# Second feed-forward: two of three chunks of the first projection as seven half-size products

## The reference, cut to what matters

```python
def swiglu(h, w_in, w_out):
    gate, up = jnp.split(h @ w_in, 2, axis=-1)
    return ((jax.nn.silu(gate) * up) @ w_out).astype(h.dtype)
...
    h = h + swiglu(rms_norm(h, ffn_norm[i]), ffn_w_in[i], ffn_w_out[i])
    h = rms_norm(h, final_norm)
```

## Time and profile before

| | |
|---|---|
| three executions | 1677.31, 1680.96, 1684.79 us |
| the profiled execution: span | 1680.7 us (its own time is not given apart from the span; 0.3 below the median) |
| TensorE busy | 1640.0 us, 98% |
| VectorE busy | 919.1 us, 55% |
| ScalarE busy | 632.4 us, 38% |
| POOL busy | 92.6 us, 6% |
| HBM traffic | 101 GB/s over the span |
| first projection of the second feed-forward | 1304.15 to 1545.40 us of the span |

### The profile page before, as it was taken

How to read it: one execution, slowest core, us unless ns; L and a number is a source line. 1 busy time by engine, 2 the same in 40 slices (tenths; PEclk the granted TensorE clock), 3 DMA queues, 4 the chain that set the end, 5 groups by cost and what they waited for, 6 DMA issues and landing times.

```text
span 1680.7 us, 20208 instructions
## 1 busy us (share of the span) xinstructions
PE 1640.0 (98%) x7941; PEld 1333.0 (79%) x7941; DVE 919.1 (55%) x1262; ACT 632.4 (38%) x816; POOL 92.6 (6%) x130
## 2 busy tenths in 40 slices
...
GB/s 320 129 119 80 44 26 51 226 164 179 160 150 151 64 102 85 101 101 77 86 103 131 86 76 52 76 65 96 97 127 75 101 100 101 100 90 66 92 104 51
DMA packets 227365, 176.71 MB, mean 105 GB/s; under 512 B 15812, under 2 KB 213316, under 8 KB 227270
## 3 DMA queue, kind: packets, MB, share of 16 engines
...
HBM read 166.84 MB, written 2.13 MB: 101 GB/s over the span
## 4 chain that ended last, share of the span: by engine, by line
PE 83%; DVE 9%; ACT 4%; issue 1%; SPq 1%; DMA 1%; DVEq 0%; POOLq 0%; POOL 0%; ACTq 0%
PE PS L477 23%; PE PS L479 23%; PE PS L478 23%; PE PS L2393 2%; PE PS L486 1%; DVE WL L92 1%; DVE T L92 1%; DMA MODW<-in_w_mod 1%; PE PS L498 1%; PE PS L500 1%; PE PS L499 1%; SPq L2682 1%; PE PS L649 1%; ACT WH L88 1%; DVE SUMS L111 1%
## 5 line engine op out<-in xcount | busy, mean ns | idle before, releaser
L477 PE MATMUL PS<-XH,WH 128*128 128x512 f32 (+2 forms) x1264 | 481.1, 381 | 3.2 <-DVE WL L92 1.1
L478 PE MATMUL PS<-XL,WH 128*128 128x512 f32 (+2 forms) x1264 | 476.8, 377 | 0.0
L479 PE MATMUL PS<-XH,WL 128*128 128x512 f32 (+2 forms) x1264 | 476.8, 377 | 0.0
L92 DVE TENSOR_TENSOR WL<-WS,WH 128x2048 fp32r<-128x2048 f32 (+3 forms) x131 | 272.8, 2083 | 209.4 <-ACT WH L88 206.6
L477 PEld LDWEIGHTS PS<-XH,WH 128*128 128x128 f32 (+1 forms) x1264 | 236.0, 187 | 48.9 <-DVE WL L92 2.0
L479 PEld LDWEIGHTS PS<-XH,WL 128*128 128x128 f32 (+1 forms) x1264 | 235.9, 187 | 44.8
L478 PEld LDWEIGHTS PS<-XL,WH 128*128 128x128 f32 (+1 forms) x1264 | 236.0, 187 | 43.2 <-issue 0.7
L88 ACT ACTIVATE WH<-WS 128x2048 fp32r<-128x2048 f32 (+3 forms) x131 | 229.1, 1749 | 76.2 <-PE PS L479 46.7
L477 PE MATMUL PS<-HH,WH 128*128 128x512 f32 x352 | 137.2, 390 | 0.2 <-DVE WL L92 0.2
L478 PE MATMUL PS<-HL,WH 128*128 128x512 f32 x352 | 136.9, 389 | 0.0
L479 PE MATMUL PS<-HH,WL 128*128 128x512 f32 x352 | 136.9, 389 | 0.0
...
## 6 DMA issues: line engine op xcount, KB each, us to landing
WS<-in_w_in SPq DMA_DIRECT2D x24, 1024.0 KB, 5.4
...
WS<-in_fox_w_in SPq DMA_DIRECT2D x16, 1024.0 KB, 5.6
...
MODW<-in_w_mod SPq DMA_DIRECT2D x8, 1024.0 KB, 11.7
```

The source lines that it names most:

```text
L92: self.e.tensor_tensor(o, a, b, op).then_inc(*self.done.to(*key))
L477: e.matmul(o, lh, rh, start=first and i == 0, stop=False)
L478: e.matmul(o, lh, rl, start=False, stop=False)
L479: ins = e.matmul(o, ll, rh, start=False, stop=last and i == n - 1)
```

## The change

Of the 22 chunks the 14 whose number is no multiple of three (`SEVEN`) are computed as a 2 x 2 block product in Strassen's way: seven products of half the terms (4) and half the tokens (256) in place of eight. A chunk is four blocks in `WS` (`blocks`): two halves of the inner dimension by gate and up. POOL makes four sums of blocks (`sums_pool`), in two buffers of rows; ScalarE and VectorE make high and low parts by units (unit 0: one block; 1 and 2: two sums each; 3: two blocks), each unit in its own place of `WH` and `WL`, taken again as soon as its last product is done (`unit_free`). Four sums of the activations (`TS`, with parts `TSH`, `TSL`) are made by VectorE and ScalarE during the output projection. The seven results lie in halves of four PSUM banks; ScalarE copies the first, and VectorE forms the sums from PSUM (`PC`, `UG`). Only the gate half is multiplied by `RST`; the up half is left unscaled, and the second projection's results are multiplied by `RST` instead, by one more VectorE instruction per tile. The other eight chunks stay whole, in two units.

The new tiles lie where x and part of the hidden rows were: x is stored in DRAM when the output projection is done and read back for the second projection (`XPARK`), and the hidden rows 5 to 12 are stored (`HPARK`), their place is taken by rows 14 to 21, and they are read back to where the activations' sums were, in time for the sixth term of the second projection. SyncE's queue issues these transfers between the weight loads (`park_load`).

The diff, cut (left out are functions that only name a cell or pass a call on, and the second projection's TensorE and ScalarE programs, which differ from the ones before by the order of the first chunk's terms and the wait for the rows read back):

```diff
@@ -297,6 +297,21 @@
     QO = zone("QO", [128, 8, L], F32R, 0)
     KO = zone("KO", [128, 8, L], F32R, 16)
+    TSH, TSL = (zone(n, [128, 4, 4, 256], F32R, k) for n, k in (("TSH", 28), ("TSL", 72)))
+    TS = zone("TS", [128, 4, 4, 256], F32, 60)
+    SA = zone("SA", [128, 4, 512], F32, 52)
+    SB = zone("SB", [128, 4, 512], F32, 88)
+    UG = zone("UG", [128, 2, 512], F32, 96)
+    PC = zone("PC", [128, 3, 256], F32, 100)
+    XPARK = nc.dram_tensor("xpark", (128, 8 * L), F32, kind="Internal").ap()
+    HPARK = [nc.dram_tensor(f"hpark{i}", (128, 8 * L), F32, kind="Internal").ap() for i in range(2)]
+    def home(f):
+        return f if f < 14 else f - 9
+    def kept(f):
+        return f + 9 if 5 <= f < 13 else home(f)
     A1, AC, A2, QG, FINV, G12, RV = 0, 8, 16, 32, 40, 48, 56
     EPSC = 143
     ST = SM[:, 128:140]
...
@@ -368,7 +386,7 @@
         arrived.append(filled[slot(j)])
     def place(j):
-        return (j - RAW + (j > GATE) + (j > GATE + 1)) % 2
+        return (j - RAW + (j > GATE) + (j > GATE + 1) + (j >= DN2)) % 2
     def stage(j):
         nk, n = chunks[j][1:3]
@@ -385,6 +403,7 @@
     freed[GATE + 1] = ("w", GATE)
     freed[GATE + 2] = ("w", GATE + 1)
     freed[GATE + 3] = ("na_values", 7)
+    freed[DN2] = ("up2", 21, 1)
     def load_chunk(e, j):
@@ -401,6 +420,11 @@
             e.wait_ge(*pe.at("w", j - 4))
         else:
             e.wait_ge(*dve.at("wl", j - 3))
+        if UP2 <= j < DN2:
+            view = stage(j).rearrange("p (x k n) -> p x k n", x=2, k=nk)
+            for x, src in parts:
+                e.dma_start(view[:, x, :, :], src).then_inc(ws_in[slot(j)], 16)
+            return
         view = stage(j).rearrange("p (k n) -> p k n", k=nk)
         for c, src in parts:
...
+    UNIT_OF = {1: (0, 0), 6: (1, 0), 5: (1, 1), 7: (2, 0), 3: (2, 1), 4: (3, 1), 2: (3, 0)}
+    PLACE_OF = {1: (0, 0), 6: (0, 256), 5: (1, 0), 7: (1, 256), 3: (2, 0), 4: (2, 256), 2: (3, 0)}
+    SEVEN = [f for f in range(22) if f % 3]
+    def seven(f):
+        return f in SEVEN
+    def unit(w, f, b):
+        p1 = place(UP2 + 1)
+        if b == 0:
+            return w[:, p1, 1536:2048] if SEVEN.index(f) % 2 else w[:, p1, 0:512]
+        return (w[:, p1, 512:1536], w[:, 1 - p1, 0:1024], w[:, 1 - p1, 1024:2048])[b - 1]
...
+    def unit_free(f, b):
+        if f == 1:
+            return "w", (UP2 - 1 if b < 2 else UP2)
+        if b == 0:
+            s = SEVEN.index(f)
+            return ("up2", SEVEN[s - 2], 1) if s > 1 else ("w", UP2 - 1)
+        if b == 3:
+            return "up2", SEVEN[SEVEN.index(f) - 1], 2
+        return "up2", f - 1, (5, 3)[b - 1] if seven(f - 1) else b
+    def hi_unit(a, f, b):
+        if not seven(f) or b in (0, 3):
+            a.e.wait_ge(ws_in[slot(UP2 + f)], arrived[UP2 + f])
+        else:
+            a.e.wait_ge(*pool.at("up2_s", f, b))
+        a.e.wait_ge(*pe.at(*unit_free(f, b)))
+        a.act(unit_cells(WH, f, b), unit_source(f, b), ACT.Copy, key=("up2_wh", f, b))
+    def lo_unit(v, f, b):
+        v.e.wait_ge(*acts.at("up2_wh", f, b))
+        v.tt(unit_cells(WL, f, b), unit_source(f, b), unit_cells(WH, f, b).bitcast(F32), ALU.subtract,
+             key=("up2_wl", f, b))
+        if b == (3 if seven(f) else 2):
+            dve.name("wl", UP2 + f)
+    def sums_pool(g, f, b):
+        st = stage(UP2 + f).rearrange("p (a n) -> p a n", a=4)
+        S = sums_of(f)
+        if b == 1:
+            g.e.wait_ge(ws_in[slot(UP2 + f)], arrived[UP2 + f])
+        if f == 2 and b == 1:
+            g.e.wait_ge(*landed("x_out"))
+        if f > 1:
+            g.e.wait_ge(*dve.at("up2_wl", SEVEN[SEVEN.index(f) - 1], b))
+        if b == 1:
+            g.tt(S[:, 1, :], st[:, 2, :], st[:, 3, :], ALU.add)
+            g.tt(S[:, 0, :], S[:, 1, :], st[:, 0, :], ALU.subtract, key=("up2_s", f, 1))
+        else:
+            g.tt(S[:, 2, :], st[:, 2, :], st[:, 0, :], ALU.subtract)
+            g.tt(S[:, 3, :], st[:, 1, :], S[:, 0, :], ALU.subtract, key=("up2_s", f, 2))
...
+    def part_pe(e, f, p):
+        b, x = UNIT_OF[p]
+        wh, wl = (unit(w, f, b)[:, 512 * x:512 * x + 512] for w in (WH, WL))
+        rh, rl = rows_of(p)
+        tm = [(wh[:, 128 * k:128 * k + 128], wl[:, 128 * k:128 * k + 128], rh[:, k, :], rl[:, k, :]) for k in range(4)]
+        prod(e, part_bank(f, p), tm, ("up2", f, p))
...
+    def up2_pe(e):
+        w, wl = (t[:, place(UP2), :].rearrange("p (x k n) -> p x k n", x=2, k=8) for t in (WH, WL))
+        e.wait_ge(*dve.at("wl", UP2))
+        tm = [terms(w[:, m], wl[:, m], 0) for m in range(2)]
+        prod_by_rows(e, [whole_bank(0, 0), whole_bank(0, 1)], tm, lambda k: dve.at("norm4", "lo", k), ("up2", 0, 2))
+        e.wait_ge(*dve.at("norm4", "sum", 7))
+        pe.name("w", UP2)
+        sums_pe(e, "norm4", T[2], L, True, True, ("norm4", "sums"), step=1)
+        for f in range(1, 22):
+            if not seven(f):
+                for m in range(2):
+                    e.wait_ge(*dve.at("up2_wl", f, m + 1))
+                    if m == 0:
+                        e.wait_ge(*dve.at("up2_done", f - 2))
+                    whole_pe(e, f, m)
+                pe.name("w", UP2 + f)
+                continue
+            e.wait_ge(*dve.at("up2_wl", f, 0))
+            if f > 2:
+                e.wait_ge(*dve.at("up2_done", f - 2))
+            part_pe(e, f, 1)
+            e.wait_ge(*dve.at("up2_wl", f, 1))
+            if f == 1:
+                e.wait_ge(*dve.at("t_lo", 3))
+            part_pe(e, f, 6)
+            if f == 2:
+                e.wait_ge(*dve.at("up2_done", 0))
+            part_pe(e, f, 5)
+            e.wait_ge(*dve.at("up2_wl", f, 2))
+            part_pe(e, f, 7)
+            if f == 1:
+                spread_pe(e, "norm4", L)
+            part_pe(e, f, 3)
+            e.wait_ge(*dve.at("up2_wl", f, 3))
+            if f == 1:
+                e.wait_ge(*dve.at("t_fourth"))
+            part_pe(e, f, 4)
+            part_pe(e, f, 2)
+            pe.name("w", UP2 + f)
...
+    def up2_act(a):
+        hi_unit(a, 1, 0)
+        hi_unit(a, 1, 1)
+        root_act(a, "norm4", L, step=1)
+        hi_unit(a, 1, 2)
+        a.e.wait_ge(*dve.at("t_fourth_full"))
+        a.act(TSH[:, 0, :, :], TS[:, 3, :, :], ACT.Copy, key=("t_fourth_hi",))
+        for f in range(1, 22):
+            if seven(f):
+                if f > 1 and not seven(f - 1):
+                    hi_unit(a, f, 2)
+                hi_unit(a, f, 3)
+                if f > 1:
+                    up2_silu_act(a, f - 1)
+                if seven(f + 1):
+                    hi_unit(a, f + 1, 0)
+                up2_copy_act(a, f)
+                hi_unit(a, f + 1, 1)
+                if f == 1:
+                    a.e.wait_ge(*pe.at("norm4", "spread"))
+                    a.act(RST[:, 0:L], bank(3), ACT.Copy, key=("norm4", "inverse"))
+                    up2_silu_act(a, 0)
+                up2_hi_act(a, f - 1)
+                hi_unit(a, f + 1, 2)
+            else:
+                up2_silu_act(a, f - 1)
+                if f < 21:
+                    hi_unit(a, f + 1, 0)
+                up2_hi_act(a, f - 1)
+                if f < 21:
+                    hi_unit(a, f + 1, 1)
+                else:
+                    hi_chunk(a, DN2)
+        up2_silu_act(a, 21)
+        up2_hi_act(a, 21)
...
+    def up2_second_dve(v, f):
+        v.e.wait_ge(*acts.at("up2_copy", f))
+        if f == 1:
+            v.e.wait_ge(*landed("x_out"))
+        v.tt(PC[:, 0, :], part_bank(f, 6), first_copy(f), ALU.add)
+    def up2_third_dve(v, f):
+        v.e.wait_ge(*pe.at("up2", f, 7))
+        v.tt(PC[:, 1:3, :], part_bank(f, 5, 512).rearrange("p (x n) -> p x n", x=2),
+             PC[:, 0, :].unsqueeze(1).broadcast_to([128, 2, 256]), ALU.add)
+        v.tt(UG[:, 1, 256:512], part_bank(f, 5), PC[:, 2, :], ALU.add)
+    def up2_first_dve(v, f):
+        e = v.e
+        if not seven(f):
+            e.wait_ge(*pe.at("up2", f, 2))
+            if f == 0:
+                e.wait_ge(*acts.at("norm4", "inverse"))
+            v.tt(up2_tile(f), whole_bank(f, 1), RST[:, 0:L], ALU.mult, key=("up2_first", f))
+            return
+        e.wait_ge(*pe.at("up2", f, 4))
+        v.tt(UG[:, :, :].rearrange("p x n -> p (x n)")[:, 256:768], part_bank(f, 3, 512),
+             PC[:, 1:3, :].rearrange("p x n -> p (x n)"), ALU.add)
+        v.tt(up2_tile(f), UG[:, 1, :], RST[:, 0:L], ALU.mult, key=("up2_first", f))
+        e.wait_ge(*pe.at("up2", f, 2))
+        v.tt(UG[:, 0, 0:256], part_bank(f, 2), first_copy(f), ALU.add, key=("up2_done", f))
+    def up2_times_dve(v, f):
+        v.e.wait_ge(*acts.at("up2_silu", f))
+        v.tt(up2_tile(f), up2_tile(f), UG[:, 0, :] if seven(f) else whole_bank(f, 0), ALU.mult, key=("up2_times", f))
+        if not seven(f):
+            dve.name("up2_done", f)
...
+    def up2_dve(v):
+        e = v.e
+        lo_unit(v, 1, 0)
+        lo_unit(v, 1, 1)
+        diagonal_dve(v, "norm4", L)
+        lo_unit(v, 1, 2)
```

(143 more changed lines are left out.)

79 lines of the change are left out of this document (54 added, 25 removed).

## The result

The changed kernel takes 1690.39 us in the median of 13 executions (1680.04 to 1693.34), the kernel before 1678.52 in 13 on the same chip (1674.45 to 1685.15): ratio 1.0054, 95% interval 1.0034 to 1.0075. The ratios in this text are estimated from all executions of both kernels; the quotient of the two medians is 1.0071 here. So the change is slower, and whether by less or by more than the bound of 0.5% stays open, as the interval reaches to both sides of it. The profiled execution took 1692.03 us, its span is 1690.2.

The account below looks back on a forecast made before the run. The prediction took TensorE to bound the kernel (busy 98% of the span): 1680.7 - 13.5 saved + 12 at the start + 6.5 steady + 0.5 read-back + 0.7 end = 1687 us; own range 1680 to 1694, 8 in 10 1671 to 1702.

Parts of the forecast that it names:

- What TensorE saves: First projection: narrow matmuls spaced 0.118 us save 0.97 us in each of 14 chunks, 13.5 us (11.2 at 0.1200).
- Exclusion of POOL and VectorE: First projection: a POOL sum and a VectorE instruction with two SBUF operands exclude each other, both sides losing in turn.
- Ahead of chunk 0: Start of first projection: tiles 4 and 5 delay chunk 0's WL, so TensorE waits 1.6 us.
- Chunk 1: Start: POOL's sums alternate with VectorE's last low parts; first product waits 4.3 us, the next 1.0 more.
- Chunk 2: Start: third product waits 1.5 us for chunk 0's bank, fourth and sixth 1.6 and 1.9 for low parts.
- Steady part: Later chunks: low part for the second chunk's sixth product late; about 1.3 us per three chunks, five groups, 6.5 us.
- Read-back: Second projection: reading parked hidden rows back takes 14.5 us, 14.3 covered; cost put at 0.5 us, ends 0 and 3.
- End: Second projection: the norm's last multiplication stands between the final matmul and the last addition, 0.7 us.
- sums slip by: Rival, faster: POOL's sums mostly meet VectorE idle or on PSUM operands; 1674 us, at best 1671; chance 0.27.
- VectorE sets the pace: Rival, slower: each POOL sum stops VectorE for 1.28 us; 22 us in place of 6.5, 1702 us; chance 0.17.
- Narrow products save nothing: Rival: narrow matmul spacing rises to 0.1295 us, kernel 1700 us; its chance is inside the slower ones.
- parked rows or gaps dear: Rival, slower: read-back costs 3 to 6 us, or waits let the granted clock fall; 1692 us; chance 0.08.

Follow-up runs that it names:

- e1: Against the changed kernel, POOL's sums replaced by constant writes, four for two sums; first-projection stage 233.85 us against 249.27, one execution 1671.07 us.
- e7: Against the changed kernel, POOL's sums replaced by six constant writes per pair, as long as the sums; first-projection stage 235.04 us against 249.27.

## Why the prediction was right, and where its steps were not

The forecast was 1687 us with its own range of 1680 to 1694, and the median is 1690.4: the mechanism as laid, a saving on TensorE eaten by late low parts. Faster, same and slower stood at 0.17, 0.45 and 0.38, with "same" the likeliest, and the interval of the result lies across the bound between "same" and slower. In these two profiles the forecast's terms came to +6.2 us, the measured ones to +11.1, and the stage took 249.3 us for some 246. That the sum came this near is in part luck: single terms were off by 2.4, 3.8 and 0.8 us one way and by 1.6 and 0.5 the other.

- **What TensorE saves: 13.5 said, 11.1 measured.** The step that failed is the choice of 0.118 for a narrow matmul. It is 0.1200, the other row and the end named for it (11.2); the "longer clean stretch" had in fact fewer steps (103 against 131). A whole chunk also takes 10.91 in place of 10.88. By the formula that the Trainium skill (TensorE: Matmul & The Clock Gate, section "Back-to-back issue gap") gives for the gap of an isolated matmul, N/2.4 + 2.5 ns, a narrow one would take an estimated 109 ns; the 0.1200 us of these rows is 11 ns more.
- **Exclusion of POOL and VectorE: right, and shown by e1 and e7.** VectorE lost 34.4 us to it, and POOL's 56 sums took 90.8 us where 1.278 each would be 71.6, so 19.2 more. Both lose in turn, as the queues were laid; the estimated 72 us for a VectorE that loses to each sum is twice what it lost.
- **Ahead of chunk 0: 1.6 said, 1.57 measured.**
- **Chunk 1: 4.3 and 1.0 said, 5.1 measured**, all at the first product (chunk 0 lasts 16.83 in place of 11.69) rather than split over two. VectorE was late one task sooner: WL of unit 0 stood behind two TSL parts, which took 3.77 us beside POOL, from 1315.47 on. (TensorE was put there at 1317.8; 1304.15 + 1.6 + 11.69 is 1317.4.)
- **Chunk 2: 5.0 said, 1.9 measured.** The step that failed is the store of the x rows: 7.6 us, not 8.9, and no product waited for chunk 0's bank; the two waits for low parts were 0.7 and 1.2 in place of 1.6 and 1.9. That the earlier landing alone made them shorter is not shown.
- **Not in the sum: the clock.** Behind the idle 5 us ahead of chunk 1 the granted clock was 0.50, the 1.2 GHz level, until 1324.86: 18 matmuls in 3.89 us where 18 x 0.12 = 2.16 would do, 1.7 lost. The prediction had this in a rival alone. Start in all: 10.4 against 12.
- **Steady part: 6.5 said, 10.3 measured.** The step that failed is the single tight deadline, at the fourth unit. In the trace the third unit is late too: 1372.48 is the fourth product, 1.35 late. The five sums were put at 4.5 us between VectorE's tasks; low parts at 1.53 to 1.60 for 1.226, and the 512-wide at 1.21 for 0.69, made more of it.
- **Read-back: 0.5 said (its own 14.5 less 14.3 is 0.2), 0 measured.** The last multiplication comes 120.82 us after the second projection's first matmul (1674.23 less 1553.41), the last addition before came 120.83 after it (1666.19 less 1545.36). DMA issues of after:

```profile
xpark<-X SPq DMA_DIRECT2D x1, 2048.0 KB, 7.6
hpark<-HH SPq DMA_DIRECT2D x1, 2048.0 KB, 6.3
hpark<-HL SPq DMA_DIRECT2D x1, 2048.0 KB, 12.1
HH<-hpark SPq DMA_DIRECT2D x1, 2048.0 KB, 8.9
HL<-hpark SPq DMA_DIRECT2D x1, 2048.0 KB, 13.3
```

  Both halves were back after 13.3 us; 14.3 were covered.
- **End: 0.7 said, 1.5 measured.** The multiplication is 0.73 as said. The other 0.78 is the last eight sums of the norm: 1.83 us at a clock of 0.52, where before they took 1.05 and the clock fell only after them.

Of the rivals, "sums slip by" was refuted by both averages, "VectorE sets the pace" by its price (22 us against 10.3). "Narrow products save nothing" was refuted by 0.1200 against 0.1295. Of "parked rows or gaps dear" the read-back cost nothing, and the fall of the clock 1.7 us.
